# Attention scores of six head pairs in three single passes instead of fp32 matmuls

## The chip, the cores and the metric

The kernel runs on one core of a Trainium2 chip. The metric is device time of one execution in microseconds. The engines are named PE (TensorE), ACT (ScalarE), DVE (VectorE), POOL (GpSimd) and SP (SyncE, which here only issues DMAs).

## The reference

Two transformer layers on 512 tokens of 1024 features, each a mixer and a gated feed-forward block with a short convolution. The first mixer is an attention with 16 heads of 64 features, over the 128 keys that an index picks for each query:

```python
q = rms_norm(q.reshape(B, S, H_A, DH_A), q_g)
k = rms_norm(k.reshape(B, S, H_A, DH_A), k_g)
...
_, idx = lax.top_k(score, topk)          # topk = min(256, S // 4) = 128
valid = idx < lim[None, :, None]
logits = jnp.einsum('bqhd,bqkhd->bhqk', qb, ks).astype(jnp.float32) * (DH_A ** -0.5)
logits = logits + bias                   # t5 bias by distance and head
logits = jnp.where(valid[:, None], logits, NEG)
p = jax.nn.softmax(logits, axis=-1).astype(vs.dtype)
return jnp.einsum('bhqk,bqkhd->bqhd', p, vs)
```

The kernel computes the scores of all keys at or before the query's chunk and adds a mask for the keys that were not picked. All inputs are fp32.

## The kernel before

Every large projection is a product of split numbers: ACT copies an fp32 tile into a rounded fp32r tile (`hi`), DVE (for a few weights POOL) writes the remainder `tile - hi` into a second one (`lo`), and PE adds hi·hi, hi·lo and lo·hi into the same PSUM bank (`product3`, lines 1911 to 1913).

The first attention, `attention(0)`, is different: its transposed queries `qT[:, i]` and keys `act[:, 8 + i]` stay fp32. A pair `i` holds two heads, in partitions 0 to 63 and 64 to 127. It is worked in three units: u = 3i + j, with j = 0 for query blocks 1 and 0 (256 and 128 keys), j = 1 for block 2 (384 keys), j = 2 for block 3 (512 keys). That makes 24 units. `scores` (line 1505) issues for each part of a unit one fp32 matmul for each head, from 64 rows of the array each (line 1520). For j = 0 the mask of the second head is first added by a bf16 matmul (line 1515).

The order of the work is written out by hand, one step per unit, on each engine:

- PE, step s: `turn(s)` transposes the probabilities of unit s (L1664), `scores(s + 3)`, then `mix(s - 1)`, probabilities by values (L1683).
- DVE, step s: `inverse_sums(s + 1)` (L1154), the copies of transposed probabilities out of PSUM (L1240; those of the second head for j = 1 and 2 are ACT's), `logits(s + 3)` (L1144: score plus bias, and the row maximum), `mask_bias(s + 4)` (L1121: bias plus mask for the first head).
- ACT, step s: the exponentials of unit s + 2 (L727), its share of the copies out (L792), the output of a finished pair when s mod 3 is 1 (`pair_out`, L798).
- POOL: `normed(u)` (L553: probabilities by the inverse sum), which waits for `inverse_sums(u)`; then `mask_bias` of the second head for units with j = 1 or 2 (L585).

Semaphores join these: `s_ok` (scores there), `l_ok` (logits there, the bank free), `r_ok`, `p_ok`, `t_ok`. After the attention `onto_residual(0, ...)` projects its output.

Of the kernel before, what the change touches and what calls it, by code (L numbers as in the profile page):

```python
# [21 lines left out]
F32 = mybir.dt.float32  # L22
# [35 lines left out]
B_DOWN = Q_LORA + KV_LORA + ROT  # L58
DB = DH + ROT
QW = H * DB  # L60

FF = 2816
FT = FF // P
# [132 lines left out]
def hybrid_layers_kernel(nc, xt, vectors, t5_bias, a_in_wide, a_in_small, a_w_out, b_w_down, b_w_uq,  # L196
# [4 lines left out]
    with ExitStack() as ctx:  # L201
# [12 lines left out]
        with ExitStack() as scope:  # L214
            sb("pad_act", [P, 6, S], F32, scope)
            c_pair = sb("c_pair", [P, 3, 2, S], F32R, scope)
            uq_hi = sb("uq_hi", [P, 2, QW], F32R, scope)
            uq_lo = sb("uq_lo", [P, 2, QW], F32R, scope)
        act = sb("act", [P, 24, S])
        vec = sb("vec", [P, V_COLS])  # L220
        con = sb("con", [P, C_COLS])
# [50 lines left out]

        with ExitStack() as scope:
            qT = sb("qT", [P, 16, S], F32, scope)
        a_hi = sb("a_hi", [P, 2, S], F32R)
        a_lo = sb("a_lo", [P, 2, S], F32R)
        u_in = sb("u_in", [P, 4, S + 4])
# [34 lines left out]
        lat_sq = qT[:, 12:16, :].rearrange("p a n -> p (a n)")[:, 0:T * B_DOWN].rearrange("p (t n) -> p t n", t=T)  # L312
        tails = act[:, 5, :].rearrange("p (j h d) -> p j h d", j=2, d=ROT)
        c_lo, c_hi = c_pair[:, :, 0, :], c_pair[:, :, 1, :]
        LAT_AT = (Q_LORA, 0, P)
        sum_q, sum_kv, sum_kr, m_tok2, m_inv, part, q_bias, s_sq, k_bias, s_kv, s_inv, kr_by = \
            (stat[:, j, :] for j in range(12))
# [19 lines left out]
        out_sem = sem("out_sem")  # L337

        x_new = {n: sem(f"x_new{n}") for n in range(1, 5)}
        hi_ok = [sem(f"hi_ok{n}") for n in range(4)]  # L340
        lo_ok = [sem(f"lo_ok{n}") for n in range(4)]
        sq_ok = sem("sq_ok")
        sq_total = sem("sq_total")
        ss_ok = sem("ss_ok")
# [32 lines left out]
        o_ok = [sem(f"o_ok{n}") for n in range(2)]  # L377
        o_out = [sem(f"o_out{n}") for n in range(2)]
        masked, masked_pool = sem("masked"), sem("masked_pool")
        toep_in = [[sem(f"toep_in{p}{e}") for e in range(2)] for p in range(2)]  # L380

        r_hi = [sem(f"r_hi{n}") for n in range(4)]
# [244 lines left out]
        def _(sc):  # L627
# [11 lines left out]
            def features_hi(n, k, gain_at):  # L639

                if n == 0:
                    sc.wait_ge(x_in[k], 16)
                else:
                    sc.wait_ge(x_new[n], ORDER[n].index(k) + 1)
                sc.activation(h_hi[:, k, :], xT[:, k, :], ACT.Identity,  # L645
                              scale=gain[:, gain_at + k:gain_at + k + 1]).then_inc(hi_ok[n], 1)
# [153 lines left out]
            def act_hi(n, kk, b, first):  # L800
# [2 lines left out]
                    sc.wait_ge(r_used[n], kk - 1)  # L803
                sc.activation(a_hi[:, b, :], act[:, kk, :], ACT.Copy).then_inc(r_hi[n], 1)

            def attention(n):
                for s in range(UNITS):
                    if s >= 4 and s % 3 == 1:
                        pair_out(n, s // 3 - 1)
                    if s == UNITS - 4:  # L810
                        act_hi(2 * n, 0, 0, True)
                    if s + 2 < UNITS:
                        exps(n, s + 2, 0)
                    if s == UNITS - 2:
                        hi((U_AOUT, U_BOUT)[n] + 1)
                        act_hi(2 * n, 1, 1, True)
                    if out_by_scalar(s, 1):
                        turned_probs(n, s, 1)
                    if s + 2 < UNITS:
                        exps(n, s + 2, 1)  # L820
                pair_out(n, PAIRS - 1)

            def onto_residual(n, u0, tiles, n_next, gain_at, nxt):
# [187 lines left out]
        def _(dve):  # L1011
# [14 lines left out]

            def prepare_lo(n, k, gain_at):

                dve.wait_ge(hi_ok[n], ORDER[n].index(k) + 1)
                dve.scalar_tensor_tensor(h_lo[:, k, :], xT[:, k, :], gain[:, gain_at + k:gain_at + k + 1],  # L1030
                                         h_hi[:, k, :].bitcast(F32), ALU.mult, ALU.subtract)\
                    .then_inc(lo_ok[n], 1)

            def total_squares(n):

# [206 lines left out]
            def act_lo(n, kk, b):  # L1242
                dve.wait_ge(r_hi[n], kk + 1)
                dve.tensor_tensor(a_lo[:, b, :], act[:, kk, :], a_hi[:, b, :].bitcast(F32), ALU.subtract)\  # L1244
                    .then_inc(r_lo[n], 1)

            def attention(n):
                for s in range(UNITS):
                    if s + 1 < UNITS:
                        inverse_sums(n, s + 1)  # L1250
                    if s == UNITS - 3:
                        act_lo(2 * n, 0, 0)
                    for e in range(2):
                        if not out_by_scalar(s, e):
                            turned_probs(n, s, e)
                    if s + 3 < UNITS:
                        logits(n, s + 3)
                    if n == 0 and s + 4 < UNITS:
                        mask_bias(s + 4)
                    if n == 1 and s == UNITS - 4:  # L1260
                        dve.wait_ge(w_lo_done, U_BOUT)
                        lo(U_BOUT)
                    if s == UNITS - 2:
                        lo((U_AOUT, U_BOUT)[n] + 1)
                        act_lo(2 * n, 1, 1)
# [226 lines left out]
        def _(pe):  # L1492
            def token_sums(n):

                bank, at = SUMS_BANK[n], SUMS_AT[n]
                pe.wait_ge(zeroed, 2)
                pe.wait_ge(sq_total, KD - 1 + n)
                pe.wait_ge(lo_ok[n], KD)
                for t in range(T):
                    ins = pe.matmul(ps[:, bank, at + t:at + t + 1], sq[:, 0, t * P:(t + 1) * P], ones[:, 0:1],  # L1500
                                    start=True, stop=True)
                ins.then_inc(ss_ok, 1)


            def scores(n, u):

# [3 lines left out]
                if n == 0:  # L1510
                    if i == 0:
                        pe.wait_ge(keep_ok, 2 + j)
                    for e in range(2):
                        if not mask_in_bias(n, u, e):
                            pe.matmul(ps[:, score_bank(u, e), 0:U_COLS[j]], ident16[:],
                                      mask[:, U_MASK[j]:U_MASK[j] + U_COLS[j]], start=True, stop=False)
                    for b, at, w in U_PARTS[j]:
                        for e in range(2):
                            part, rows = slice(e * DH, (e + 1) * DH), slice(b * P, (b + 1) * P)
                            ins = pe.matmul(ps[:, score_bank(u, e), at:at + w], qT[part, i, rows],  # L1520
                                            act[part, 8 + i, 0:w], start=mask_in_bias(n, u, e),
                                            stop=mask_in_bias(n, u, e) or at + w == U_COLS[j])
                            if at + w == U_COLS[j]:
                                ins.then_inc(s_ok[n], 1)
# [37 lines left out]
            for k in range(KD):  # L1562
                if k == 3:
                    pe.wait_ge(b_in, 16 * 2)
                    pe.matmul(ps[0:H, 5, :], t5, bucket[:, 0:512], start=True, stop=True)
                    pe.matmul(ps[0:H, 6, 0:128], t5, bucket[:, 512:640], start=True, stop=True).then_inc(rows_mm, 1)
                pe.wait_ge(lo_ok[0], k + 1)
                if k % 4 == 3:
                    pe.wait_ge(w_lo_done, 3 + k // 4)
                else:  # L1570
# [177 lines left out]
            def feed_forward(l):  # L1748
# [29 lines left out]
                for j, k in enumerate(ORDER[n]):  # L1778
                    if j == 4:
                        pe.wait_ge(w_lo_done, U_UP[l] + 1)  # L1780

                    pe.wait_ge(lo_ok[n], j + 1)
# [32 lines left out]
            for j in range(4):  # L1815
                if j == 2:
                    pe.wait_ge(w_lo_done, U_B + 1)
                for t in (2, 3, 0, 1):

                    pe.wait_ge(lo_ok[2], max(j + 1, ORDER[2].index(t)))  # L1820
                    ins = down(j, t)
            ins.then_inc(pb_half, 1)
            pe.wait_ge(w_lo_done, U_B + 2)
            for t in range(T):
                for k in range(4, KD):
                    if t == 0:
                        pe.wait_ge(lo_ok[2], k + 1)
                    ins = down(k, t)
                ins.then_inc(pb_done, 1)
                if t == 1:  # L1830
# [149 lines left out]
```

## Time and profile before

| | us |
|---|---|
| median of three runs | 1225.16 (1224.37 to 1225.64) |
| the profiled execution, its own time | 1226.64 |
| its span (first to last instruction) | 1224.8 |
| the first attention, steady part, five pairs | 207.24 to 248.41 |

PE is busy in 1205.8 us of the span (98%), DVE in 764.7 (62%), ACT in 545.4 (45%), POOL in 170.5 (14%). These shares are averages over stages that have different limits; within the first attention DVE, ACT and POOL are far busier than that. An fp32 matmul is shown as two MATMUL records, an fp32r or bf16 matmul as one. A record's own duration overlaps that of the next, so what an instruction occupies is read from the start of one row to the start of the next.

### The profile page before, as it was taken

Reading aid. Unit: us, or ns where it says so; the run is one execution under the profiler, and the core shown is the slowest. Engines: PE = TensorE matmul, PEld = TensorE weight load, DVE = VectorE, ACT = ScalarE, POOL = GpSimd, SP = SyncE. Lnnn points to the kernel's source line nnn. Section 1 sums busy time; section 2 is a strip of 40 time slices with the busy share of each in tenths; the row PEclk is TensorE's granted clock in tenths of the full one; section 3 lists DMA queues with packets and bytes.
Section 4 is the critical chain, followed back from the end, with each engine's and each line's share of the span. In section 5 each row is a group of like instructions: output and inputs, shape, how many; then the busy total and the mean of one; then the engine's idle time right before and its main releaser. Section 6 shows DMA issues by size and latency. Waiting matters only on the chain.

```text
span 1224.8 us, 17141 instructions
## 1 busy us (share of the span) xinstructions
PE 1205.8 (98%) x6046; PEld 970.9 (79%) x6046; DVE 764.7 (62%) x1344; ACT 545.4 (45%) x896; POOL 170.5 (14%) x239
## 2 busy tenths in 40 slices
PE   9999999999999999999999889999999999999998
PEld 7858886678888888888888876778888888888887
DVE  5588987946766566663336887654766656664334
ACT  5554336745443343432236577643643334333322
POOL 0523436720000000000000524430000000000000
PEclk9999999999999999999999999999999999999999
DMA  7522121212232222213233200004222122212332
GB/s 268 164 88 98 70 96 61 71 52 103 103 121 85 103 103 100 88 52 103 87 101 104 73 19 1 1 35 138 103 104 103 68 103 103 103 51 88 100 101 105
DMA packets 26400, 110.83 MB, mean 90 GB/s; under 512 B 2880, under 2 KB 3264, under 8 KB 19184
## 3 DMA queue, kind: packets, MB, share of 16 engines
q1 hardware_dynamic: 26352, 110.21, 26.2%
q8 instruction: 28, 0.46, 0.2%
q14 instruction: 20, 0.16, 0.0%
HBM read 108.06 MB, written 6.33 MB: 93 GB/s over the span
## 4 chain that ended last, share of the span: by engine, by line
PE 90%; DVE 4%; ACT 2%; issue 1%; POOL 1%; DMA 1%; SPq 0%; DVEq 0%; POOLq 0%; ACTq 0%
PE ps L1911 26%; PE ps L1913 26%; PE ps L1912 26%; PE ps L1683 3%; PE ps L1664 3%; PE ps L1528 3%; PE ps L1520 2%; PE ps L1648 1%; PE ps L1550 1%; DVE hs L1418 1%; POOL probs L553 0%; DVE tok L1441 0%; DMA raw<-in_a_in_wide 0%; ACT h_hi L645 0%; DVE act L1224 0%
## 5 line engine op out<-in xcount | busy, mean ns | idle before, releaser
L1024 DVE TENSOR_TENSOR w_lo<-raw,w_hi 128x1024 fp32r<-128x1024 f32 (+2 forms) x109 | 181.0, 1660 | 255.6 <-ACT w_hi L637 255.6
L1911 PE MATMUL ps<-h_hi,w_hi 128*128 128x512 f32 x704 | 274.2, 390 | 0.0
L1912 PE MATMUL ps<-h_lo,w_hi 128*128 128x512 f32 x704 | 273.9, 389 | 0.0
L1913 PE MATMUL ps<-h_hi,w_lo 128*128 128x512 f32 x704 | 273.9, 389 | 0.0
L637 ACT ACTIVATE w_hi<-raw 128x1024 fp32r<-128x1024 f32 (+2 forms) x120 | 173.0, 1441 | 220.1 <-PE ps L1913 220.1
L1911 PE MATMUL ps<-a_hi,w_hi 128*128 128x512 f32 x480 | 187.7, 391 | 0.6 <-DVE a_lo L1244 0.6
L1912 PE MATMUL ps<-a_lo,w_hi 128*128 128x512 f32 x480 | 186.8, 389 | 0.0
L1913 PE MATMUL ps<-a_hi,w_lo 128*128 128x512 f32 x480 | 186.8, 389 | 0.0
L1912 PEld LDWEIGHTS ps<-h_lo,w_hi 128*128 128x128 f32 x704 | 132.2, 188 | 27.5
L1911 PEld LDWEIGHTS ps<-h_hi,w_hi 128*128 128x128 f32 x704 | 132.1, 188 | 27.4
L1913 PEld LDWEIGHTS ps<-h_hi,w_lo 128*128 128x128 f32 x704 | 132.1, 188 | 27.1
L860 ACT ACTIVATE cv<-u_in,vec 128x512 f32<-128x512 f32 x88 | 71.5, 816 | 182.0 <-DVE u_in L1308 179.8
L1308 DVE TENSOR_TENSOR u_in<-ps,rbc 128x512 f32<-128x512 f32 x88 | 60.2, 688 | 86.2 <-PE ps L1913 83.4
L1911 PEld LDWEIGHTS ps<-a_hi,w_hi 128*128 128x128 f32 x480 | 90.1, 188 | 21.6 <-issue 1.7
L1913 PEld LDWEIGHTS ps<-a_hi,w_lo 128*128 128x128 f32 x480 | 90.1, 188 | 18.9
L1912 PEld LDWEIGHTS ps<-a_lo,w_hi 128*128 128x128 f32 x480 | 90.1, 188 | 18.2
L1911 PE MATMUL ps<-w_hi,h_hi 128*128 128x512 f32 (+1 forms) x248 | 100.0, 403 | 1.9 <-DVE w_lo L1060 1.9
L1913 PE MATMUL ps<-w_hi,h_lo 128*128 128x512 f32 (+1 forms) x248 | 96.4, 389 | 0.0
L1912 PE MATMUL ps<-w_lo,h_hi 128*128 128x512 f32 (+1 forms) x248 | 96.1, 387 | 0.0
L553 POOL TENSOR_SCALAR probs<-probs,inv_sum 128x256 f32<-128x256 f32 (+3 forms) x128 | 68.3, 549 | 83.1 <-DVE inv_sum L1154 83.0
L727 ACT ACTIVATE probs<-probs,neg_max 128x256 f32<-128x256 f32 (+3 forms) x128 | 70.5, 554 | 13.0 <-DVE neg_max L1144 12.7
L1315 DVE SCALAR_TENSOR_TENSOR cv<-u_in,vec,cv 128x512 f32<-128x512 f32 x88 | 63.9, 747 | 12.8 <-ACT cv L860 12.8
(199 smaller groups left out, 1478.8 us busy)
## 6 DMA issues: line engine op xcount, KB each, us to landing
raw<-in_f_up SPq DMA_DIRECT2D x44, 1024.0 KB, 4.8
raw<-in_f_w_down SPq DMA_DIRECT2D x44, 512.0 KB, 3.3
raw<-in_a_in_wide SPq DMA_DIRECT2D x12, 1024.0 KB, 4.9
bias_tiles<-bias_rows SPq DMA_DIRECT2D x1, 4096.0 KB, 20.1
raw<-in_a_w_out SPq DMA_DIRECT2D x8, 512.0 KB, 3.3
raw<-in_b_w_out SPq DMA_DIRECT2D x8, 512.0 KB, 3.2
xT<-in_xt SPq DMA_DIRECT2D x8, 256.0 KB, 6.7
raw<-in_a_in_wide SPq DMA_DIRECT2D x8, 256.0 KB, 6.8
```

The source lines that it names most:

```text
L553: ins = pool.tensor_scalar(x, x, inv_sum[:, slot, e, p:p + 1], 1.0, ALU.mult, ALU.mult)
L637: sc.activation(w_hi[:, s, 0:n], raw[:, s, 0:n], ACT.Copy).then_inc(w_hi_done, 1)
L727: ins = sc.activation(x, x, ACT.Exp, bias=neg_max[:, slot, e, p:p + 1], scale=-1.0, accum_out=sums[:, slot, e, p:p + 1])
L860: sc.activation(cv[:, q, :], u_in[:, q, 2:2 + S], ACT.Identity, bias=conv[:, 3, bass.ds(ch, 1)], scale=conv[:, 2, bass.ds(ch, 1)])\
L1024: dve.tensor_tensor(w_lo[:, s, 0:n], raw[:, s, 0:n], w_hi[:, s, 0:n].bitcast(F32), ALU.subtract)\
L1308: dve.tensor_tensor(u_in[:, q, 2:2 + S], ps[:, 4 + q, :], rbc[:], ALU.mult).then_inc(f_in[l], 1)
L1315: dve.scalar_tensor_tensor(cv[:, q, :], u_in[:, q, 1:1 + S], conv[:, 1, bass.ds(ch, 1)], cv[:, q, :], ALU.mult, ALU.add).then_inc(f_t1[l], 1)
L1528: ins = pe.matmul(ps[:, score_bank(u, e), at:at + w], qT[0:DB, 2 * i + e, b * P:(b + 1) * P], act[0:DB, 8 + 2 * i + e, 0:w], start=True, s ...
L1664: ins = pe.transpose(ps[:, turn_bank(u, e), c * P:(c + 1) * P], probs[slot][:, e, c * P:(c + 1) * P], ident)
L1911: pe.matmul(dst, s_hi, m_hi, start=start, stop=False)
L1912: pe.matmul(dst, s_hi, m_lo, start=False, stop=False)
L1913: return pe.matmul(dst, s_lo, m_hi, start=False, stop=stop)
```

## The change

For pairs 2 to 7, units 6 to 23, the fp32 matmuls of the scores are replaced. ACT rounds the pair's keys and queries (128x512 each) into the halves of `w_hi` that the output weights don't use, two buffers in turn; DVE writes the remainders over the fp32 queries and keys, in place; PE takes three fp32r passes for each part and head: hi·hi, lo·hi, hi·lo, with the two heads in turn in the two row halves of the array. Pairs 0 and 1 stay fp32. Pair p's rounding stands in ACT's step 3(p - 2), its query remainder in DVE's step 3(p - 2) + 1, its key remainder in DVE's step 3(p - 2) + 2, and PE needs both in its step 3(p - 2) + 3. Besides, the semaphores `hi_ok` and `lo_ok` of the four norm stages become one each, with counts that go on; the waits stay at the same events.

```diff
+def pair_to_split(s):
+    return s // 3 + A_SPLIT_FROM if s % 3 == 0 and s // 3 + A_SPLIT_FROM < PAIRS else None
...
+        aq_hi, ak_hi = w_hi[:, :, D:D + S], w_hi[:, :, D + S:SLOT]
+        aq_lo, ak_lo = qT_lo[:, 0:PAIRS], act_lo[:, PAIRS:2 * PAIRS]
...
+            def pair_hi(i):                                   # ACT
+                if i >= A_SPLIT_FROM + 2:
+                    sc.wait_ge(s_ok[0], 6 * (i - 1))
+                sc.activation(ak_hi[:, i % 2, :], act[:, 8 + i, :], ACT.Copy).then_inc(heads_hi, 1)
+                sc.activation(aq_hi[:, i % 2, :], qT[:, i, :], ACT.Copy).then_inc(heads_hi, 1)
...
                     if s + 2 < UNITS:
                         exps(n, s + 2, 1)
+                    if n == 0 and pair_to_split(s):
+                        pair_hi(pair_to_split(s))
...
+            def pair_queries_lo(i):                           # DVE
+                dve.wait_ge(heads_hi, 2 * (i - A_SPLIT_FROM) + 2)
+                dve.tensor_tensor(aq_lo[:, i, :], qT[:, i, :], aq_hi[:, i % 2, :].bitcast(F32), ALU.subtract)\
+                    .then_inc(heads_q_lo, 1)
+            def pair_keys_lo(i):
+                dve.wait_ge(heads_hi, 2 * (i - A_SPLIT_FROM) + 1)
+                dve.tensor_tensor(ak_lo[:, i, :], act[:, 8 + i, :], ak_hi[:, i % 2, :].bitcast(F32),
+                                  ALU.subtract).then_inc(heads_k_lo, 1)
...
                     if s + 3 < UNITS:
                         logits(n, s + 3)
+                    if n == 0 and s and pair_to_split(s - 1):
+                        pair_queries_lo(pair_to_split(s - 1))
+                    if n == 0 and s > 1 and pair_to_split(s - 2):
+                        pair_keys_lo(pair_to_split(s - 2))
                     if n == 0 and s + 4 < UNITS:
                         mask_bias(s + 4)
...
+            def three_passes(u, b, at, w):                    # PE
+                i, last = u // 3, at + w == U_COLS[u % 3]
+                rows = slice(b * P, (b + 1) * P)
+                q_passes = (aq_hi[:, i % 2, rows], aq_lo[:, i, rows], aq_hi[:, i % 2, rows])
+                k_passes = (ak_hi[:, i % 2, 0:w], ak_hi[:, i % 2, 0:w], ak_lo[:, i, 0:w])
+                for p in range(3):
+                    for e in range(2):
+                        part, alone = slice(e * DH, (e + 1) * DH), mask_in_bias(0, u, e)
+                        ins = pe.matmul(ps[:, score_bank(u, e), at:at + w], q_passes[p][part], k_passes[p][part],
+                                        start=alone and p == 0, stop=p == 2 and (alone or last))
+                        if p == 2 and last:
+                            ins.then_inc(s_ok[0], 1)
...
+                    if i >= A_SPLIT_FROM and j == 0:
+                        pe.wait_ge(heads_q_lo, i - A_SPLIT_FROM + 1)
+                        pe.wait_ge(heads_k_lo, i - A_SPLIT_FROM + 1)
                     for b, at, w in U_PARTS[j]:
+                        if i >= A_SPLIT_FROM:
+                            three_passes(u, b, at, w)
+                            continue
```

DVE before, from the logits of a unit with j = 1 to the first mask and bias of the next pair (line numbers of each kernel's own file; ISA is the instruction that adds the bias and takes the maximum):

```order
L1144 ISA probs,neg_max<-ps,act 128x384 [waits masked,s_ok0]
L1144 ISA neg_max 128x1
L1144 ISA probs,neg_max<-ps,act 128x384 [waits masked_pool,s_ok0]
L1144 ISA neg_max 128x1
L1121 TENSOR_TENSOR act<-toep_b,mask 128x512
L1154 RECIPROCAL inv_sum<-sums 128x4 [waits e_ok0]
L1240 COPY probsT<-ps 128x512 [waits t_ok0]
L1144 ISA probs,neg_max<-ps,act 128x512 [waits masked,s_ok0]
L1144 ISA neg_max 128x1
L1144 ISA probs,neg_max<-ps,act 128x512 [waits masked_pool,s_ok0]
L1144 ISA neg_max 128x1
L1121 TENSOR_TENSOR act<-rope_tmp,mask 128x256 [waits toep_in00]
```

and the same stretch of DVE now:

```order
L1166 ISA probs,neg_max<-ps,act 128x384 [waits masked_pool,s_ok0]
L1166 ISA neg_max 128x1
L1272 TENSOR_TENSOR qT_lo<-qT,w_hi 128x512 [waits heads_hi]
L1143 TENSOR_TENSOR act<-rope_tmp,mask 128x512
L1176 RECIPROCAL inv_sum<-sums 128x4 [waits e_ok0]
L1262 COPY probsT<-ps 128x512 [waits t_ok0]
L1166 ISA probs,neg_max<-ps,act 128x512 [waits masked,s_ok0]
L1166 ISA neg_max 128x1
L1166 ISA probs,neg_max<-ps,act 128x512 [waits masked_pool,s_ok0]
L1166 ISA neg_max 128x1
L1278 TENSOR_TENSOR act_lo<-act,w_hi 128x512 [waits heads_hi]
L1143 TENSOR_TENSOR act<-toep_b,mask 128x256 [waits toep_in10]
```

Two TENSOR_TENSOR of 128x512 came in for each pair, each between the logits and the mask and bias that follow them.

PE before, the scores of a unit with j = 0:

```order
L1515 MATMUL ps<-mask,ident 128x384 [waits l_ok0]
L1520 MATMUL ps<-act,qT 128x256 x2
L1520 MATMUL ps<-act,qT 128x128 x2
L1683 MATMUL ps<-probsT,v 64x128 [waits pt_dve0,pt_act0]
L1683 MATMUL ps<-probsT,v 64x128 x7
```

and now:

```order
L1567 MATMUL ps<-mask,ident 128x384 [waits l_ok0]
L1552 MATMUL ps<-w_hi 128x256 [waits heads_k_lo,heads_q_lo]
L1552 MATMUL ps<-w_hi 128x256
L1552 MATMUL ps<-w_hi,qT_lo 128x256 x2
L1552 MATMUL ps<-act_lo,w_hi 128x256 x2
L1552 MATMUL ps<-w_hi 128x128 x2
L1552 MATMUL ps<-w_hi,qT_lo 128x128 x2
L1552 MATMUL ps<-act_lo,w_hi 128x128 x2
L1741 MATMUL ps<-probsT,v 64x128 [waits pt_dve0,pt_act0]
```

Four matmuls became twelve, and the first of them now waits for both remainders.

## Rows read from the trace of the kernel before

**Rows 1.** The page: busy time of the engines; the chain that ended last.

```profile
PE 1205.8 (98%) x6046; PEld 970.9 (79%) x6046; DVE 764.7 (62%) x1344; ACT 545.4 (45%) x896; POOL 170.5 (14%) x239
PE ps L1911 26%; PE ps L1913 26%; PE ps L1912 26%; PE ps L1683 3%; PE ps L1664 3%; PE ps L1528 3%; PE ps L1520 2%; PE ps L1648 1%; PE ps L1550 1%; DVE hs L1418 1%; POOL probs L553 0%; DVE tok L1441 0%; DMA raw<-in_a_in_wide 0%; ACT h_hi L645 0%; DVE act L1224 0%
```

**Rows 2.** Busy time in five stretches, one pair each, clock at the end.

```profile
core 0: us, PE busy (x) PEld busy (x) DVE busy (x) ACT busy (x) POOL busy (x), PEclk, DMA share, GB/s
207.24:215.45 8.21, 8.21 (x80) 5.59 (x79) 7.41 (x28) 6.02 (x19) 6.10 (x10) 1.00 0.22 67
...
sum 41.17, PE 41.17 PEld 27.94 DVE 37.73 ACT 30.27 POOL 30.65; mean PE 8.23 PEld 5.59 DVE 7.55 ACT 6.05 POOL 6.13
```

**Rows 3.** Chain that ended last, one pair: start, us, what.

```profile
207.24 1.06 PE ps L1520 x4
208.30 0.81 PE ps L1683 x12
...
209.91 0.16 PE ps L1515
210.07 0.85 PE ps L1520 x8
...
212.75 0.85 PE ps L1520 x4
213.60 0.81 PE ps L1683 x12
```

**Rows 4.** Waits from 204 to 250 us: waiting and waited for, us, times, longest.

```profile
DVE probs L1144 <- PE ps L1520: 3.9, 6, 0.7
```

**Rows 5.** DVE in order of time: start, duration, instruction, idle before.

```profile
231.17 0.69 DVE L1121 TENSOR_TENSOR act<-toep_b,mask 128x512 f32<-128x512 f32 x1
231.77 0.17 DVE L1154 RECIPROCAL inv_sum<-sums 128x4 f32<-128x4 f32 x1
231.86 0.66 DVE L1240 COPY probsT<-ps 128x512 f32<-128x512 f32 x1
233.10 0.69 DVE L1144 CUSTOM_DVE_ANT_0 probs<-ps,act 128x512 f32<-128x512 f32 x1 [0.59 <-PE ps L1520]
...
233.72 0.69 DVE L1144 CUSTOM_DVE_ANT_0 probs<-ps,act 128x512 f32<-128x512 f32 x1
234.33 0.08 DVE L1144 DVE_READ_ACCUMULATOR2_ANT neg_max<- 128x1 f32 x1
```

**Rows 6.** DVE in order of time, the last remainder of the attention.

```profile
250.90 0.67 DVE L1244 TENSOR_TENSOR a_lo<-act,a_hi 128x512 fp32r<-128x512 f32 x1
251.49 1.01 DVE L1240 COPY probsT<-ps 128x384 f32<-128x384 f32 x2
```

**Rows 7.** DVE in order of time, early and late in the attention.

```profile
199.51 0.69 DVE L1144 CUSTOM_DVE_ANT_0 probs<-ps,act 128x512 f32<-128x512 f32 x1 [0.75 <-PE ps L1520]
...
200.74 1.34 DVE L1121 TENSOR_TENSOR act<-rope_tmp,mask 128x256 f32<-128x256 f32 x2
...
242.62 0.62 DVE L1121 TENSOR_TENSOR act<-toep_b,mask 128x256 f32<-128x256 f32 x2
```

**Rows 8.** POOL in order of time, two stretches.

```profile
200.68 0.91 POOL L585 TENSOR_TENSOR act<-toep_a,mask 128x384 f32<-128x384 f32 x1
...
232.04 1.62 POOL L553 TENSOR_SCALAR probs<-probs,inv_sum 128x256 f32<-128x256 f32 x4 [0.89 <-DVE inv_sum L1154]
233.63 0.92 POOL L585 TENSOR_TENSOR act<-toep_a,mask 128x384 f32<-128x384 f32 x1
```

**Rows 9.** PE in order of time, single-pass products of 512 columns.

```profile
299.84 0.39 PE L1913 MATMUL ps<-a_hi,w_lo 128*128 128x512 f32 x1
300.06 0.39 PE L1911 MATMUL ps<-a_hi,w_hi 128*128 128x512 f32 x1
300.29 0.39 PE L1912 MATMUL ps<-a_lo,w_hi 128*128 128x512 f32 x1
```

**Rows 10.** PE chain, six transposes of 128 columns.

```profile
209.11 0.80 PE ps L1664 x6
```

**Rows 11.** ACT: a rounding copy (ns min/median/max); two rows in order of time.

```profile
L804 ACT ACTIVATE a_hi<-act x60: 613/614/625, 247.6 to 1211.7; 128x512 fp32r x52, 128x512 fp32r<-128x512 f32 x8
235.17 0.19 ACT L727 ACTIVATION_READ_ACCUMULATOR probs<-probs,neg_max 128x1 f32 x1
236.67 0.60 ACT L798 ACTIVATE act<-ps 128x512 f32<-128x512 f32 x1 [1.31 <-PE ps L1683]
```

**Rows 12.** Groups of DVE, 204 to 250 us: count, busy us, mean ns.

```profile
L1121 DVE TENSOR_TENSOR act<-toep_b,mask 128x384 f32<-128x384 f32 x3 | 2.5, 844 | 0.0
```

More of the change, by code:

```diff
@@ L60 @@
 QW = H * DB
+A_SPLIT_FROM = 2
 FF = 2816
@@ L218, in hybrid_layers_kernel @@
             uq_lo = sb("uq_lo", [P, 2, QW], F32R, scope)
+        with ExitStack() as scope:
+            act_lo = sb("act_lo", [P, 24, S], F32R, scope)
         act = sb("act", [P, 24, S])
@@ L274, in hybrid_layers_kernel @@
             qT = sb("qT", [P, 16, S], F32, scope)
+        with ExitStack() as scope:
+            qT_lo = sb("qT_lo", [P, 16, S], F32R, scope)
         a_hi = sb("a_hi", [P, 2, S], F32R)
@@ L339, in hybrid_layers_kernel @@
         x_new = {n: sem(f"x_new{n}") for n in range(1, 5)}
-        hi_ok = [sem(f"hi_ok{n}") for n in range(4)]
-        lo_ok = [sem(f"lo_ok{n}") for n in range(4)]
+        hi_ok = sem("hi_ok")
+        lo_ok = sem("lo_ok")
         sq_ok = sem("sq_ok")
@@ L379, in hybrid_layers_kernel @@
         masked, masked_pool = sem("masked"), sem("masked_pool")
+        heads_hi, heads_q_lo, heads_k_lo = sem("heads_hi"), sem("heads_q_lo"), sem("heads_k_lo")
         toep_in = [[sem(f"toep_in{p}{e}") for e in range(2)] for p in range(2)]
@@ L645, in features_hi @@
                 sc.activation(h_hi[:, k, :], xT[:, k, :], ACT.Identity,
-                              scale=gain[:, gain_at + k:gain_at + k + 1]).then_inc(hi_ok[n], 1)
+                              scale=gain[:, gain_at + k:gain_at + k + 1]).then_inc(hi_ok, 1)
             def square_of(n, k):
@@ L1027, in prepare_lo @@
             def prepare_lo(n, k, gain_at):
-                dve.wait_ge(hi_ok[n], ORDER[n].index(k) + 1)
+                dve.wait_ge(hi_ok, KD * n + ORDER[n].index(k) + 1)
                 dve.scalar_tensor_tensor(h_lo[:, k, :], xT[:, k, :], gain[:, gain_at + k:gain_at + k + 1],
                                          h_hi[:, k, :].bitcast(F32), ALU.mult, ALU.subtract)\
-                    .then_inc(lo_ok[n], 1)
+                    .then_inc(lo_ok, 1)
             def total_squares(n):
@@ L1497, in token_sums @@
                 pe.wait_ge(sq_total, KD - 1 + n)
-                pe.wait_ge(lo_ok[n], KD)
+                pe.wait_ge(lo_ok, KD * (n + 1))
                 for t in range(T):
@@ L1566, in _ @@
                     pe.matmul(ps[0:H, 6, 0:128], t5, bucket[:, 512:640], start=True, stop=True).then_inc(rows_mm, 1)
-                pe.wait_ge(lo_ok[0], k + 1)
+                pe.wait_ge(lo_ok, k + 1)
                 if k % 4 == 3:
@@ L1780, in feed_forward @@
                         pe.wait_ge(w_lo_done, U_UP[l] + 1)
-                    pe.wait_ge(lo_ok[n], j + 1)
+                    pe.wait_ge(lo_ok, KD * n + j + 1)
                     for q in range(2):
@@ L1818, in _ @@
                 for t in (2, 3, 0, 1):
-                    pe.wait_ge(lo_ok[2], max(j + 1, ORDER[2].index(t)))
+                    pe.wait_ge(lo_ok, 2 * KD + max(j + 1, ORDER[2].index(t)))
                     ins = down(j, t)
@@ L1826, in _ @@
                     if t == 0:
-                        pe.wait_ge(lo_ok[2], k + 1)
+                        pe.wait_ge(lo_ok, 2 * KD + k + 1)
                     ins = down(k, t)
```

## The prediction, made before the changed kernel ran

> **What bounds the kernel now.** I read the page first. PE is busy for 1205.8 us of the 1224.8, and the chain that ended last is PE for nine tenths; the scores' line, L1520, has 2% of it [rows 1]. That says PE is the bound on average, not what bounds the stage that is changed. So the second view is busy time by stretch, one pair of heads to a stretch. In the steady part of the first attention a pair takes 8.23 us, PE is busy for all of it, DVE for 7.55, ACT for 6.05 and POOL for 6.13, at a granted clock of 1.00 [rows 2]. The chain there is nothing but PE instructions [rows 3]. PE is the bound, but DVE has only 8.23 - 7.55 = 0.68 us to spare in a pair. The view of waits says where that is: between 204 and 250 us DVE waits for L1520 six times, 3.9 us in total [rows 4], once a pair, ahead of the logits of the j = 2 unit [rows 5].
>
> Times below are differences to the profiled execution (1226.64 us, span 1224.8 and 1.84 around it). It is 1.5 us above the median, so I add the difference to the median, 1225.16.
>
> **What PE saves.** A unit's fp32 scores take 0.85 us with 384 columns and 1.06 with 512 [rows 3]. The 128 columns between them cost 0.21 us. Both heads run at once, or it would be twice that. Per column that is 0.21 / 128, so the 384 columns of a j = 1 or j = 0 unit account for 0.64 us and the 512 for 0.85, and 0.21 us of each unit is a fixed part for getting into and out of the row halves, which stays. A single pass of 512 columns takes 0.227 us, start to start [rows 9]. Three passes in row halves, both heads at once: 0.21 + 3 x 0.227 = 0.89 for j = 2 (saves 0.17) and 0.21 + 3 x 0.17 = 0.72 for j = 1 (saves 0.13). For j = 0 there are short instructions: no single fp32r pass of 256 or 128 columns is in the trace. The nearest rows are the fp32 transposes of 128 columns, 0.80 / 6 = 0.13 us each [rows 10], so I take 0.13 for each of the six: 0.21 + 6 x 0.13 = 0.99, 0.14 more than now. Bounds: as fast as the columns of the 512 pass, 0.21 + 3 x 0.17 = 0.72; or, for a 128-column pass, what 128 columns of fp32 cost, 0.21 [rows 3], and 0.13 for the other, 1.23. Over a pair PE saves 0.17 + 0.13 - 0.14 = 0.16 us, between +0.43 and -0.08. For six pairs that is 1.0 us, between 2.6 and -0.5. It reaches the end of the kernel only if PE stays the bound.
>
> **What DVE gets.** Two remainders of 128x512 a pair. The same form at the end of this attention occupies DVE from 250.90 to 251.49, 0.59 us [rows 6]. Twelve of them are 7.1 us. In a pair, DVE goes to 7.55 + 2 x 0.59 = 8.73 us against 8.23 for the pair now and 8.1 for PE after the change. So DVE becomes the bound and PE's gain is lost behind it. What DVE can absorb is its waits for the scores: 3.9 us [rows 4] and the 0.75 ahead of the logits of unit 5 [rows 7], together 4.65. What is left is 7.1 - 4.65 = 2.45 us.
>
> **What POOL does to it.** A key remainder stands right behind the logits of the j = 2 unit and ahead of a mask and bias. Without its wait, DVE would leave the copy at 231.86 + 0.58 = 232.44, and the two logits of 0.61 each at 233.67 [rows 5]. POOL starts its own mask and bias, L585, at 233.63 and takes 0.92 [rows 8]; it hangs on the inverse sums of the same DVE step, so the distance stays. The trace has this meeting once: at 200.74 DVE starts its two mask and bias instructions 0.06 us behind L585 of POOL, and they take 1.34 us, against 0.62 at 242.62 where POOL's is nearly over [rows 7, 8]. The meeting costs 0.72 us. In the steady part it isn't there today, because the wait for the scores takes DVE past it; the overlap that is left there costs up to 0.09. For pair 2 it is already in the trace (the 1.34). For pairs 3 to 7 it is new: 5 x (0.72 - 0.09) = 3.15 us. Bounds: nothing, with DVE getting in first and POOL waiting where nobody waits for POOL; or the whole 0.92 five times, 4.6 us. I take 3.15, as the row for it is this very pair of instructions. The query remainders fall where POOL has finished `normed` and is idle, and cost nothing beyond their length.
>
> The Trainium skill, "SBUF — State Buffer", section "Who interferes with whom", has a rule for this: a DVE instruction with two SBUF inputs and a GpSimd instruction that reads SBUF exclude each other for a whole instruction, and whichever was issued first wins. The rows at 200.74 agree (0.72 us lost to an instruction of 0.91). By the rule alone a key remainder that arrives 0.04 us late waits for nearly all of the 0.92, and the sum would be 5 x 0.88 in place of 5 x 0.63.
>
> **What ACT gets.** Two rounding copies of 0.61 us [rows 11], 1.2 us a pair, in the step before `pair_out`. ACT is idle there for 1.31 us, waiting for PE [rows 11]. They fit, and with longer pairs the more so. If that cover were gone, ACT at 6.05 + 1.2 = 7.3 us a pair would still be below DVE. Only the first, in step 0, has no `pair_out` behind it and can make the exponentials of unit 3 up to 0.6 us late; 0 to 0.6, I take 0.
>
> **The new waits.** PE waits for the key remainder ahead of the j = 0 scores; behind it on PE stand those scores, the mix of the unit before and the next transposes. DVE itself waits for these scores next, but first has a mask and bias and two copies (0.62 and 1.01 us long) [rows 6, 7], against 0.99 for the scores. PE catches up within that, so this wait moves PE's idle time and adds none to the pair. ACT's wait for `s_ok` is for scores that are long done. The one `hi_ok` and `lo_ok` wait for the same events: nothing, either side.
>
> **The sum.** 2.45 + 3.15 = +5.6 us: a pair goes from 8.23 to about 9.35 us for pairs 3 to 7, and 1225.16 + 5.6 = 1230.8 us. The rest of the kernel shifts as a whole: after the attention PE is the bound again and nothing was moved there.
>
> **The rivals.**
> - *DVE is the bound, but isn't held by POOL* (DVE gets its instructions in first, or the two fall apart by a tenth of a microsecond). The margin is 0.04 us, so this is open. Then +2.45, less up to 0.09 x 5 for the overlap that goes: 1225.16 + 2.2 = 1227.4. Chance 0.18.
> - *The two heads don't overlap in fp32r.* Nothing in the trace shows two single passes in row halves. Then the scores' streams double to 2 x (0.51 + 0.51 + 0.68) = 3.4 us a pair with no short-instruction loss, or 3.9 with it, in place of 0.64 + 0.64 + 0.85 = 2.13. PE is at 8.23 + 1.3 to 1.8 = 9.5 to 10.0 us a pair and bounds it with DVE close behind: six pairs of +1.3 to +1.8, 8 to 11 us, about 1234.5. The fp32 scores do overlap [rows 3], which speaks against. Chance 0.10.
> - *PE stays the bound* (the other side, not slower). The place is DVE's wait for L1520 in each pair: the remainders hide in it if the two together take no more than 0.68 + what PE keeps. With the range of PE's gain that needs a remainder below (0.68 - 0.16) / 2 = 0.26 us, against 0.59. The price would be PE's alone: -1.0, down to -2.6, so 1224.2. For it speaks only that some DVE durations contain waiting for POOL (0.84 for a mask and bias of 384 against 0.69 for one of 512) [rows 5, 12], which could shrink. Chance 0.07.
>
> **How the numbers follow.** The forecast, DVE bound and held by POOL, 0.62; the rivals 0.18, 0.10 and 0.07; 0.03 for anything else. The time is that of the likeliest, 1230.8. Its own range, with the bounds of the meeting and of ACT's first copies, is 1227.2 to 1232.9. The overall range takes in most of the first rival and part of the second: 1226.9 to 1233.6. A change of 0.2% is 2.45 us, about what a measurement can tell from none, so slower means above 1227.6. The forecast and the second rival lie there, and a third of the first: 0.78. Within 0.2% lie the rest of the first, and most of the third: 0.19. Faster: 0.03.
>
> **What the changed kernel's profile will show.** In a stretch of one pair from about 210 to 250 us: length 9.2 to 9.5, DVE busy over 9 us with the wait for the scores gone from the list, PE idle for over 1 us a pair, mostly ahead of the j = 0 scores (waiting for the key remainder, L1278) and ahead of the transposes (waiting for POOL's `normed`). L1278 should be seen at about 1.3 us where L1272 has 0.67. The scores of a j = 2 unit should occupy 0.89. ACT should show no new wait. It is wrong if DVE still waits for the scores in each pair, if L1278 is as short as L1272, or if the scores of a j = 2 unit take over 1.1 us.

## The result, and the profile of the changed kernel

The changed kernel takes longer, by about as much as was forecast.

| | before | after |
|---|---|---|
| median of 4 and 4 runs | 1225.40 us (1224.37 to 1225.65) | 1232.24 us (1231.58 to 1233.35) |
| ratio, 95% interval | | 1.0058 [1.0046, 1.0071] |
| profiled execution, span | 1226.64 us, 1224.8 us | 1231.97 us, 1230.2 us |
| first inverse sum to the last one, first attention | 66.88 us | 73.25 us |
| one pair of heads, between the same inverse sums | 8.19 to 8.35 us | 9.31 to 9.34 us |

The fourth row is the difference of the start times of the first and the last of the 24 reciprocals that DVE computes there, one per unit; the fifth is the distance between reciprocals three units apart, in the steady part (units 7 to 20). They say where the time is: 73.25 - 66.88 = 6.4 us are in this stretch, against 6.84 between the medians. The spans of the two profiled executions differ by only 5.4 us: in the one of after the first inverse sum comes 1.5 us earlier (184.02 against 185.54), for reasons that lie ahead of it, and the part behind the last one is 0.5 us longer. So I count inside the stretch, not between the spans.

The page, first part and chain, answers to [rows 1]:

```profile
PE 1204.8 (98%) x6094; PEld 972.3 (79%) x6094; DVE 775.4 (63%) x1356; ACT 551.2 (45%) x908; POOL 170.6 (14%) x239
PE 86%; DVE 8%; ACT 2%; issue 2%; DMA 1%; POOL 1%; SPq 0%; DVEq 0%; ACTq 0%; POOLq 0%
```

PE's total fell by 1.0 us from that in [rows 1] and its share stayed 98%. Whoever reads only the totals sees no reason for a longer kernel. Busy time by stretch, one pair each, answers to [rows 2] (columns as there):

```profile
208.43:217.76 9.33, 8.38 (x88) 6.04 (x86) 9.33 (x30) 7.07 (x21) 6.15 (x11) 1.00 0.18 57
217.76:227.08 9.32, 8.38 (x88) 6.04 (x86) 9.32 (x32) 7.07 (x21) 6.13 (x11) 1.00 0.19 58
...
sum 27.97, PE 25.14 PEld 18.10 DVE 27.97 ACT 21.22 POOL 18.42; mean PE 8.38 PEld 6.03 DVE 9.32 ACT 7.07 POOL 6.14
```

DVE has no idle time left: 9.32 of 9.32 us. PE, which filled its pair before, now stands still for 9.32 - 8.38 = 0.94 us. DVE in order of time, within one such pair, answers to [rows 5]:

```profile
224.53 0.68 DVE L1272 TENSOR_TENSOR qT_lo<-qT,w_hi 128x512 fp32r<-128x512 f32 x1
...
226.46 0.69 DVE L1166 CUSTOM_DVE_ANT_0 probs<-ps,act 128x512 f32<-128x512 f32 x1
...
227.08 0.69 DVE L1166 CUSTOM_DVE_ANT_0 probs<-ps,act 128x512 f32<-128x512 f32 x1
...
227.69 1.37 DVE L1278 TENSOR_TENSOR act_lo<-act,w_hi 128x512 fp32r<-128x512 f32 x1
228.98 0.61 DVE L1143 TENSOR_TENSOR act<-toep_b,mask 128x256 f32<-128x256 f32 x2
```

The logits (L1166) follow the copy without a wait; the 0.59 us of [rows 5] are gone. The query remainder L1272 takes 0.68. The key remainder L1278 does the same work on a tile of the same size and takes 1.37. POOL at that moment, answers to [rows 8]:

```profile
226.00 1.62 POOL L566 TENSOR_SCALAR probs<-probs,inv_sum 128x256 f32<-128x256 f32 x4 [1.34 <-DVE inv_sum L1176]
227.59 0.92 POOL L598 TENSOR_TENSOR act<-toep_b,mask 128x384 f32<-128x384 f32 x1
```

POOL's mask and bias starts at 227.59 and ends at 228.51. DVE's remainder is issued at 227.69 and runs in effect from then: 228.51 + 0.60 = 229.1. DVE is occupied by it from 227.69 to 228.98, 1.29 us in place of 0.60. The duration of a row here holds time in which the instruction stood still; only its neighbours on the other engine tell that. The Trainium skill, "SBUF — State Buffer", section "Who interferes with whom", says that it is issue order that decides who blocks; here POOL was 0.10 us ahead, and DVE lost 0.69 us, three quarters of POOL's instruction. That POOL held DVE agrees; a loss of all that was left of POOL's instruction would have been 0.82 us, and the measured one is less. DVE's logits, which read the scores from PSUM and so have one input in SBUF, aren't held: at 230.51, ahead of a mask and bias of POOL, and at 231.06, beside it (POOL's runs from 230.88 to 232.04), the 256 columns take 0.41 us both times.

The waits from 204 to 256 us, answers to [rows 4]:

```profile
PE ps L1552 <- DVE act_lo L1278: 3.7, 5, 0.8
...
DVE probs L1166 <- PE ps L1552: 0.6, 1, 0.6
```

The direction has turned: DVE waited for PE's scores six times, 3.9 us; now PE waits for DVE's key remainder five times, 3.7 us. The one wait of DVE that is left is the last. The chain that ended last, pieces in order of time (start, us, what), answers to [rows 3]:

```profile
246.43 1.29 DVE act_lo L1278
247.72 0.14 issue
247.86 0.91 PE ps L1552 x12
248.77 1.02 PE ps L1741 x16
249.79 0.80 PE ps L1722 x6
250.60 0.72 PE ps L1552 x6
...
253.42 0.89 PE ps L1552 x4
```

These are the three kinds of unit in the three-pass form: 0.91 us for j = 0, 0.72 for j = 1, 0.89 for j = 2, where [rows 3] have 0.85, 0.85 and 1.06. Both heads still run at once. From 247.86 on, the chain leaves DVE and stays on PE.

### The profile page after: what moved, and what is told of

Its sections match the earlier page's. It is cut to its first block, busy times and chain, and to the rows that moved or that the text cites. A ratio compares the mean times of both kernels' runs of the same rounds, so it can differ in the third digit from the quotient of the medians.

```text
span 1230.2 us, 17267 instructions
## 1 busy us (share of the span) xinstructions
PE 1204.8 (98%) x6094; PEld 972.3 (79%) x6094; DVE 775.4 (63%) x1356; ACT 551.2 (45%) x908; POOL 170.6 (14%) x239
## 4 chain that ended last, share of the span: by engine, by line
PE 86%; DVE 8%; ACT 2%; issue 2%; DMA 1%; POOL 1%; SPq 0%; DVEq 0%; ACTq 0%; POOLq 0%
PE ps L1969 26%; PE ps L1971 26%; PE ps L1970 25%; PE ps L1586 3%; PE ps L1741 2%; PE ps L1722 2%; DVE probs L1166 1%; DVE act L1143 1%; PE ps L1706 1%; DVE hs L1456 1%; DVE act_lo L1278 1%; PE ps L1608 1%; PE ps L1552 1%; DVE tok L1479 1%; DMA raw<-in_a_in_wide 0%
```

## The experiments

All times are medians, ratios are against the kernel before on the same chip (its median there 1224.85 to 1225.01 us). "Length" is the stretch from the first to the last inverse sum, 66.88 us before and 73.25 after.

**What PE gains by itself.** No remainders; all three passes multiply the rounded copies (that is what it leaves out), and PE waits for ACT's rounding alone. So PE and ACT have the work of the changed kernel and DVE that of the kernel before.

```diff
-                    if n == 0 and s and pair_to_split(s - 1):
-                        pair_queries_lo(pair_to_split(s - 1))
-                    if n == 0 and s > 1 and pair_to_split(s - 2):
-                        pair_keys_lo(pair_to_split(s - 2))
...
-                q_passes = (aq_hi[:, i % 2, rows], aq_lo[:, i, rows], aq_hi[:, i % 2, rows])
-                k_passes = (ak_hi[:, i % 2, 0:w], ak_hi[:, i % 2, 0:w], ak_lo[:, i, 0:w])
+                q_passes = (aq_hi[:, i % 2, rows],) * 3
+                k_passes = (ak_hi[:, i % 2, 0:w],) * 3
```

> The changed kernel without DVE's twelve remainders: PE takes the same three passes per part and head, all of them over the rounded copies (so the product is hi x hi three times), ACT rounds as in the change. Theory (DVE's work is the whole loss): PE is the bound again, and a pair takes 8.23 - 0.23 = 8.0 us, since the passes occupy 0.92, 0.72 and 0.89 us against 0.85, 0.85 and 1.06 of the fp32 scores; the kernel is 1.4 us faster than before, about 1224.0. Rival (the passes, the row halves or ACT's rounding carry part of the loss): slower than before, with pairs over 8.3 us.

Measured: 1223.89 us, ratio 0.9992 [0.9983, 1.0002]; a pair takes 8.13 to 8.14 us, length 66.18. DVE in order of time:

```profile
222.21 0.69 DVE L1166 CUSTOM_DVE_ANT_0 probs<-ps,act 128x512 f32<-128x512 f32 x1 [0.58 <-PE ps L1548]
222.83 0.69 DVE L1166 CUSTOM_DVE_ANT_0 probs<-ps,act 128x512 f32<-128x512 f32 x1
223.44 0.70 DVE L1143 TENSOR_TENSOR act<-toep_b,mask 128x256 f32<-128x256 f32 x2
```

DVE's wait is back at its old size, and with it the short mask and bias. The whole loss is gone, so it hangs on the twelve remainders. PE's gain by itself is 0.1 us a pair and about 1 us in all (1224.85 - 1223.89; 0.7 us of it in the stretch), which its interval doesn't quite tell from nothing. I had expected pairs of 8.0 us. The chain, which is all PE here, says where the rest is:

```profile
211.79 0.60 PE ps L1717 x4
212.42 0.63 PE ps L1717 x4
...
215.72 0.84 PE ps L1548 x12
```

The scores save 0.31 us a pair (0.89, 0.84 and 0.72 us against 1.06, 0.85 and 0.85). But the eight transposes ahead of the scores for j = 2 take 1.26 us with their gap, and in the kernel before the same eight take 1.03 to 1.12 us in five of six pairs:

```profile
214.41 1.04 PE ps L1664 x8
```

So the transposes take back 0.2 of the 0.3 us. What makes them longer no run here shows.

**What the remainders cost by themselves.** The kernel before, with twelve instructions of the same kind on DVE at the places of the remainders. Nobody waits for them, and PE and ACT are as before.

```diff
+            def extra(s):
+                if 1 <= s < 18 and s % 3:
+                    i = s // 3 + 2
+                    at = D if s % 3 == 1 else D + S
+                    dve.tensor_tensor(w_hi[:, i % 2, at:at + S], qT[:, i, :], act[:, 8 + i, :], ALU.subtract)
```

> The kernel before with nothing but twelve extra subtractions of 128x512 on DVE, at the places of the remainders; their results go where nobody reads them, nobody waits for them, and PE and ACT do what they did. Theory (DVE's work is the whole loss, and POOL's mask and bias blocks the second of each pair): as slow as the changed kernel, +6.6 us, about 1232, with pairs of 9.3 us and the second subtraction at 1.36 us. Rival (the loss needs PE's new wait for the key remainder): +3 us or less.

Measured: 1232.37 us, ratio 1.0057 [1.0041, 1.0074]; a pair 9.31 to 9.33 us, length 73.66: the changed kernel's numbers. DVE, the instructions added, then POOL:

```profile
224.92 0.68 DVE L1251 TENSOR_TENSOR w_hi<-qT,act 128x512 fp32r<-128x512 f32 x1
...
228.24 1.20 DVE L1251 TENSOR_TENSOR w_hi<-qT,act 128x512 fp32r<-128x512 f32 x1
```

```profile
227.98 0.92 POOL L585 TENSOR_TENSOR act<-toep_b,mask 128x384 f32<-128x384 f32 x1
```

So PE's new wait for the key remainder costs nothing of its own that can be seen; it shows where PE's idle time went. PE's gain of 1 us isn't seen either. Here DVE's logits start 0.79 us after the copy, in place of 0.64 (the profile names the scores for it at 217.70). So DVE comes 0.26 us behind POOL in place of 0.10, and its instruction is shorter by as much, 1.20 in place of 1.37. From DVE's inverse sums for four columns to the end of POOL's mask and bias it is 2.77 us in both kernels (226.13 to 228.90 here, 225.74 to 228.51 in the changed one), and DVE is past its subtraction 0.46 and 0.47 us after that. What sets this part of the pair is the way from DVE over POOL back to DVE; an arrival 0.16 us later costs nothing.

**POOL's part.** Four kernels ask what the meeting with POOL is worth. The first moves the key remainder to the place right behind the query remainder:

```diff
-                    if n == 0 and s > 1 and pair_to_split(s - 2):
-                        pair_keys_lo(pair_to_split(s - 2))
+                        pair_keys_lo(pair_to_split(s - 1))
```

> The changed kernel with the key remainder moved one step ahead, right behind the query remainder, where POOL is idle; PE no longer waits for it. Theory (whatever two-input instruction DVE has when POOL starts L598 is blocked): the key remainder takes 0.68 us, but the mask and bias behind the j = 2 logits now takes 1.3 or more in place of 0.61, and the time stays that of the changed kernel within 0.7 us, 1231.5 to 1232.9. Rival (the key remainder is slow by itself, by what it reads or writes, or PE's wait for it costs): 4 to 5 us faster than the changed kernel, about 1227.5.

Measured: 1231.39 us, 0.1 us below the range that I had given, ratio 1.0052 [1.0035, 1.0068]; pair 9.33 us, length 73.45.

```profile
224.88 0.68 DVE L1278 TENSOR_TENSOR act_lo<-act,w_hi 128x512 fp32r<-128x512 f32 x1
...
227.96 1.37 DVE L1143 TENSOR_TENSOR act<-toep_b,mask 128x256 f32<-128x256 f32 x2
```

The remainder is short now, and the mask and bias behind the logits stands still in its place. It isn't the remainder that is slow: it is whatever two-input instruction DVE issues there. The second kernel leaves the changed kernel's order and cuts POOL's mask and bias for the j = 1 units to 16 columns:

```diff
                 (b, at, w), at0 = U_PARTS[j][0], U_MASK[j]
+                w = 16 if j == 1 else w
```

> The changed kernel with POOL's mask and bias of the j = 1 units cut to 16 of 384 columns (the second head's mask is left incomplete there), same instructions otherwise. Theory (POOL blocks the key remainder for 0.77 us, six times): the key remainder takes 0.68 us, a pair 8.55 us, and the kernel is 6 x 0.77 = 4.6 us faster than the changed one, about 1227.6. Rival (the key remainder is slow by itself): no change, 1232.

Measured: 1227.39 us, ratio 1.0021 [1.0011, 1.003]; pair 8.62 to 8.65 us, length 69.90.

```profile
225.69 0.69 DVE L1279 TENSOR_TENSOR act_lo<-act,w_hi 128x512 fp32r<-128x512 f32 x1
226.29 0.62 DVE L1144 TENSOR_TENSOR act<-toep_b,mask 128x256 f32<-128x256 f32 x2
```

Same instruction, same place, 0.69 us. The pair is 0.7 us shorter, the length 3.4 (73.25 - 69.90), the median 4.9 (1232.24 - 1227.39), or 4.3 if each is counted from the kernel before on its own chip (6.84 - 2.54). The third cuts the j = 2 units' mask and bias as well (`w = 16`), and a fourth makes that cut in the kernel before, as a control.

> The changed kernel with both of POOL's masks and biases of a pair cut to 16 columns (the second head's mask is left incomplete for j = 1 and 2). Theory (a shared access of DVE and POOL): the key remainder's 0.77 us goes six times, the 0.28 us that DVE's mask and bias for j = 1 loses goes too, and so does the 0.97 us that the one for unit 5 lost behind the query remainder of pair 2: a pair takes 8.27 us, and the kernel is 7 us faster than the changed one, about 1225. Rival (only the meeting with the key remainder counts): as e4, about 1227.5.

> The kernel before with the same cut of POOL's masks and biases. Theory (before, PE bounds the pair and DVE has a wait of 0.65 us to take the loss): nothing, within 0.7 us of before. Rival (POOL's work costs in both kernels alike, by whatever way): 3 to 7 us faster than before.

Measured: 1225.96 us, ratio 1.0008 [0.9999, 1.0017], pair 8.52, length 68.37; and 1223.94 us, ratio 0.9990 [0.9981, 0.9999], pair 8.19, length 66.16. The time of the first fell as expected within a microsecond, but its pair is 0.25 us longer than I expected; with POOL out of the way DVE is busy for 8.42 us of the 8.52 by its own work, and I had put that too low. The control shows that the cut is worth 1.1 us even without the remainders, where I had expected less than 0.7. If the cut by itself is worth no more in the changed kernel, at least 3.2 of the 4.3 us above belong to the meeting. The price of the change with POOL's two instructions cut is 1225.96 - 1223.94 = 2.0 us, against 6.84 with them whole. Between the two lie 4.8 us, the price of DVE and POOL meeting (by the lengths 2.2 against 6.4, so 4.2).

**Half of the change.** If the loss is DVE's lack of room, then one remainder in a pair instead of two should fit into DVE's 0.6 us of waiting. In this kernel only pairs 3, 5 and 7 are split, with the key remainder a pair ahead of the query's, both behind the logits of a j = 1 unit, away from POOL.

```diff
-A_SPLIT_FROM = 2
+A_SPLIT = (3, 5, 7)
...
-                    if n == 0 and s > 1 and pair_to_split(s - 2):
-                        pair_keys_lo(pair_to_split(s - 2))
+                    if n == 0 and s >= 4 and pair_to_split(s - 4):
+                        pair_keys_lo(pair_to_split(s - 4))
```

> Only pairs 3, 5 and 7 are split, and their two remainders are spread over two pairs of DVE's steps, both behind the logits of a j = 1 unit, where POOL is idle: one remainder of 0.60 us in each pair, against the wait of 0.65 us for the scores. Theory (the change loses by what DVE gets beyond its wait): DVE keeps up, its wait shrinks to 0.1 us or less, no mask and bias is blocked, and PE gives back its 0.23 us three times: 0.3 to 0.7 us faster than before, 1224.3, hardly to be told from it. Rival (a remainder costs its length wherever it stands): 3 us slower than before.

Measured: 1228.10 us, ratio 1.0026 [1.0017, 1.0036]; pair 8.72 us, length 69.93. My theory was wrong by 3.8 us, and the time is that of the rival, 3 us above the kernel before (1228.10 - 1225.01 = 3.1). DVE in order of time, then POOL:

```profile
208.49 1.14 DVE L1143 TENSOR_TENSOR act<-toep_b,mask 128x256 f32<-128x256 f32 x2
...
213.90 0.68 DVE L1272 TENSOR_TENSOR qT_lo<-qT,w_hi 128x512 fp32r<-128x512 f32 x1
...
217.05 1.30 DVE L1143 TENSOR_TENSOR act<-rope_tmp,mask 128x256 f32<-128x256 f32 x2
```

```profile
208.23 0.92 POOL L598 TENSOR_TENSOR act<-toep_b,mask 128x384 f32<-128x384 f32 x1
...
216.95 0.92 POOL L598 TENSOR_TENSOR act<-toep_a,mask 128x384 f32<-128x384 f32 x1
```

The remainder did fit into the wait. But then DVE comes out of the logits earlier, 0.10 and 0.26 us behind POOL in turn instead of 0.7, and its mask and bias takes 1.30 and 1.14 us, where it has 0.62 at 242.62 [rows 7] and 0.70 at 234.33 in the kernel before. There, DVE's wait for PE is what carries it past most of POOL's instruction. It looks like slack and isn't: what fills it brings on a stall of 0.5 to 0.7 us, about as long as the wait. POOL's start hangs on DVE's inverse sums (the wait in brackets at 226.00 above), so POOL moves along and the meeting comes back in every pair. So the rival had the price but not the reason: the remainder's own length is hidden, and the stall isn't. This reads the rows; the same kernel with POOL's masks cut, which would settle it by a time, wasn't run.

**POOL's instruction moved away.** The changed kernel, with POOL's mask and bias of the j = 1 unit issued one unit later, beside that of the j = 2 unit.

```diff
-                ahead = u + (3 if u < 3 else 4)
-                if 3 < ahead < UNITS and ahead % 3:
-                    mask_bias(ahead)
+                if u < 3:
+                    later = (u + 3,) if u else ()
+                else:
+                    later = (u + 3, u + 4) if u % 3 == 1 else ()
+                for ahead in later:
+                    if ahead < UNITS:
+                        mask_bias(ahead)
```

> The changed kernel, and POOL's mask and bias for a j = 1 unit is issued one normed() later, behind the probabilities of the j = 1 unit, from pair 2 on. No work is left out. POOL is then idle when DVE comes to the key remainder; two masks and biases of POOL stand in a row in the next step, 2.08 us, where DVE has 2.1 us of copies and logits out of PSUM first. Theory (what costs is which POOL instruction runs when DVE issues a two-input one): the key remainder takes 0.68 us for pairs 3 to 7, DVE's mask and bias for j = 1 loses at most what it loses now or a little more, a pair takes 8.6 us, and the kernel is 3.5 us faster than the changed one, 1228.5. Rival (the exclusion only moves: DVE's or POOL's next instruction loses the same 0.7): no change, 1232.

Measured: 1236.19 us, ratio 1.0089 [1.0074, 1.0105]; pair 10.17 to 10.27 us, length 78.11. Theory and rival are both wrong, and on the other side. DVE, POOL, and the waits from 204 to 250 us:

```profile
218.74 0.69 DVE L1170 CUSTOM_DVE_ANT_0 probs<-ps,act 128x512 f32<-128x512 f32 x1 [1.61 <-PE ps L1556]
...
219.97 0.69 DVE L1282 TENSOR_TENSOR act_lo<-act,w_hi 128x512 fp32r<-128x512 f32 x1
```

```profile
214.64 3.90 POOL L566 TENSOR_SCALAR probs<-probs,inv_sum 128x512 f32<-128x512 f32 x6
...
222.47 2.36 POOL L598 TENSOR_TENSOR act<-toep_a,mask 128x384 f32<-128x384 f32 x2
```

```profile
DVE probs L1170 <- PE ps L1556: 8.0, 5, 1.6
PE ps L1726 <- POOL probs L566: 8.0, 10, 1.1
```

The key remainder is short, as expected. But POOL's two masks, now together 2.36 us, stand in front of `normed` of the next unit; PE waits for that ahead of its transposes (1.1 us), the scores behind them are late, and DVE waits 1.6 us for these. I had counted POOL as free because it is busy for only 6.1 us a pair; what counts is that its `normed` is on PE's path. That is read from these rows. Two more kernels take this apart: the same move on top of the every-second-pair kernel, and on the kernel before.

> Pairs 3, 5 and 7 split with one remainder in each pair, as in e7, and POOL's mask and bias for j = 1 issued later, as in e8. Theory: without the meeting DVE keeps up with PE, and PE's 0.23 us a split pair comes through: 0 to 0.7 us faster than before, 1224.6. Rival (the exclusion only moves): as e7, 1228.

> The kernel before with POOL's mask and bias for j = 1 issued later, as in e8. Theory (PE bounds the pair before, and no remainder meets POOL): no change, within 0.5 us of before. Rival (two masks and biases of POOL in a row delay normed() and with it PE's transposes): 1 to 4 us slower.

Measured: 1228.54 us, ratio 1.0028 [1.0017, 1.0039], 17.7 us for two pairs, length 70.84; and 1227.80 us, ratio 1.0023 [1.0014, 1.0032], pair 8.77, length 69.74. Both of my theories fell, and both times the time is that of the rival (1228, and 1 to 4 us slower). In the kernel before, the move alone costs 2.9 us (1227.80 - 1224.90): the delay of `normed`, without any remainder. That alone would be most of the 3.6 us that the other kernel loses, so its time doesn't prove that the meeting moved; its rows show that one is there. It has gone from one mask and bias to another, and in the pair before to a query remainder:

```profile
213.59 1.06 DVE L1276 TENSOR_TENSOR qT_lo<-qT,w_hi 128x512 fp32r<-128x512 f32 x1
...
219.99 1.50 DVE L1147 TENSOR_TENSOR act<-rope_tmp,mask 128x384 f32<-128x384 f32 x1
```

The last is 1.50 us for an instruction that took 0.84 before; POOL's pair of masks ran from 219.04 to 221.08. None of the orders that I tried is free of both, the stall between DVE and POOL and a late `normed`, and none with the whole computation is faster than the kernel before.

## Why the prediction was right, and where its terms were off

The mechanism held in its main steps: DVE, held by POOL, becomes the bound; the scores' wait goes in all pairs but the last; the key remainder meets POOL; PE's gain is lost behind DVE; ACT is not in it. By its own steps:

- *PE's saving.* 0.89 and 0.72 us were forecast for j = 2 and j = 1, and measured. For j = 0 I took 0.99, from 0.13 us for each short pass; it is 0.91 to 0.92 in the changed kernel, behind PE's wait, and 0.84 in the kernel without remainders, where nothing holds it. So it saves 0.01 us and doesn't cost 0.14. Behind the first pass, the 256-column and 128-column passes start 0.12 and 0.06 to 0.12 us apart. PE in order of time, two heads in each row:

```profile
229.20 0.39 PE L1552 MATMUL ps<-w_hi 64*128 64x256 f32 x2 [0.75 <-DVE act_lo L1278]
229.39 0.31 PE L1552 MATMUL ps<-w_hi,qT_lo 64*128 64x256 f32 x2
229.51 0.31 PE L1552 MATMUL ps<-act_lo,w_hi 64*128 64x256 f32 x2
229.63 0.25 PE L1552 MATMUL ps<-w_hi 64*128 64x128 f32 x2
229.69 0.31 PE L1552 MATMUL ps<-w_hi,qT_lo 64*128 64x128 f32 x2
229.80 0.30 PE L1552 MATMUL ps<-act_lo,w_hi 64*128 64x128 f32 x2
```

  PE was to save 1.0 us; the kernel without remainders gave 1.0. That the two agree is luck: the scores save 0.31 us a pair, twice the 0.16 of the forecast, and the transposes, which the forecast didn't touch, take 0.2 back. The gain never reached the end, as forecast. That the two heads overlap in this form was the second rival's question, and settles it.
- *A pair.* Forecast "about 9.35" us, measured 9.31 to 9.34. The terms of the forecast's sum make 2 x 0.59 - 0.65 (a sixth of the 3.9 us of waits) + 0.63 = 1.16 us a pair, so 9.39. From the inverse sums of unit 4 to those of unit 19 the traces have 5 x 1.09 us (46.62 against 41.16), which is -0.35 us.
- *The meeting with POOL.* Forecast 0.72 us, from the one place in the trace where a mask and bias stood still [rows 7]; measured 1.29 - 0.60 = 0.69. The other sum of the prediction, 5 x 0.88, takes the whole rest of POOL's instruction and would have been too much; besides, it doesn't take off the 0.09 that the 0.63 beside it has taken off. The first rival (DVE gets in first) fell by 0.10 us of distance; that this distance is set by DVE's own inverse sums was in the working, and is why it came out at 0.10 us in five pairs (0.03 in pair 2).
- *Pair 2.* Here a term was mis-sized. I took the stall already in the trace for this pair and added only the remainders' length, 0.45 us after its 0.75 us of waiting. It lost 1.3 (12.49 us in place of 11.18 between the inverse sums of units 1 and 4). The query remainder pushes the next mask and bias behind POOL's (DVE, then POOL):

```profile
195.60 0.68 DVE L1272 TENSOR_TENSOR qT_lo<-qT,w_hi 128x512 fp32r<-128x512 f32 x1
...
196.20 1.64 DVE L1143 TENSOR_TENSOR act<-toep_b,mask 128x512 f32<-128x512 f32 x1
```

```profile
195.70 1.60 POOL L598 TENSOR_TENSOR act<-toep_b,mask 128x512 f32<-128x512 f32 x1
```

  POOL is itself held by the remainder (1.60 in place of 1.16; in the kernel before DVE's mask and bias held it as long), goes next, and DVE's following instruction waits for it: 1.64 us in place of 0.68. That the query remainders "cost nothing beyond their length" was right for five pairs of six. +0.87 us.
- *The last wait.* I let the remainders absorb all 4.65 us of DVE's waits. The last one stays:

```profile
254.45 0.69 DVE L1166 CUSTOM_DVE_ANT_0 probs<-ps,act 128x512 f32<-128x512 f32 x1 [0.58 <-PE ps L1552]
```

  Ahead of it no remainder stands, and PE, held 0.75 us by the last key remainder, is behind and runs from 247.86 on with no gap over 0.04 us. In the forecast's sum it was to give back 0.65 us (5.6 - 0.45 - 5 x 1.16); what came back from unit 19 on is 0.17 us, the length by which the scores ahead of it are shorter. +0.48 us.
- *The sum.* 5.6 + 0.87 + 0.48 - 0.35 = 6.6 us; the stretch grew by 6.4 and the medians by 6.84. The missing 0.2 us lie between the inverse sums of units 0 and 1, ahead of the first remainder (5.04 us against 5.28). What is left between 6.4 and 6.84 is within the spread of the runs.
- *PE's idle time.* Over 1 us a pair was said, ahead of the j = 0 scores and of the transposes. The places are right, the size is 0.94: 3.7 us in five waits for the key remainder, and 0.15 to 0.16 a pair for POOL's `normed`.
- *ACT.* Its two rounding copies raised it from 6.05 to 7.07 us a pair and it got no new wait for them.
- *The third rival*, PE stays the bound, needed a remainder of 0.26 us. It took 0.60 to 1.29.

## What to carry to other kernels

Where an engine's wait is to be filled with new work, ask first what the wait carries it past. A wait can keep two engines apart that cannot run certain instructions at the same time, and then filling it can cost the wait's length a second time. Add up, for one period, the instructions of both engines that hold each other up, and follow what hangs behind each instruction of the other engine before moving it: a low share of busy time does not make its order free.

## What the runs showed of the hardware

- At 195.60 to 197.77 DVE and POOL take turns, one instruction each: DVE loses 0.96 us to an instruction of POOL that was itself held up by DVE's previous one. Two DVE instructions of this kind in a row didn't keep POOL out there.
- When DVE came 0.10 or 0.26 us behind POOL's mask and bias, it was done at the same distance from POOL's end, 0.47 and 0.46 us.
- In row halves, a pass of rounded copies over 128 columns costs 0.06 to 0.12 us for both heads together, less than the 0.13 us of a full-height fp32 transpose of 128 columns [rows 10], by which I had priced it. Without a wait ahead of it the group of twelve takes 0.84 us, no more than the 0.85 of the fp32 scores.
- Cutting POOL's masks in the kernel before gave 1.1 us, in a kernel where PE is busy for the whole of each steady pair; two thirds of it (66.88 - 66.16 = 0.7 us) lie in this stretch. Why is not shown.
